# State groups taken in pairs, and projections in whole fp32, in the stage of the states

## What is computed

```python
xn = rmsnorm(h, norm1_g)
proj = xn @ w_in
u, q, k, v, qi, ki, wi, g_ssm, g_attn = split(proj)   # 512, 512, 128, 128, 256, 32, 8, 1024, 1024 columns
# s5_branch: 32 groups of 16 channels and 64 complex states
bu = einsum('gpc,bsgc->bsgp', b_bar, u)
states = associative_scan(a_bar * s + bu)             # over the 256 tokens
y = real(einsum('gcp,bsgp->bsgc', c, states)) + d_skip * u
y = gelu(y); y = y * sigmoid(y @ w_glu)
# dsa_branch: rotation of q, k, qi, ki; then for each token the 64 keys with the highest index score
score = sum_h(relu(qi_h @ ki.T) * wi_h); sel = top_k(score, 64); softmax attention over sel
h = h + (sigmoid(g_ssm) * (y @ w_ssm_up) + sigmoid(g_attn) * (y_attn @ w_attn_up)) @ w_out
```

## Time and profile before

| | us |
|---|---|
| three runs | 1834.30, 1828.82, 1832.76; median 1832.76 |
| the profiled execution | 1834.04, its span 1832.2 |
| granted TensorE clock, mean | 0.967 |
| TensorE matmul / weight load busy | 94% / 82% |
| VectorE, ScalarE, GpSimd busy | 65%, 47%, 41% |
| HBM over the span | 154 GB/s |

### The profile page before, as it was taken

The page is one execution under the profiler, slowest core; times in us unless marked ns, Lnnn a source line. Parts: engine busy times, 40 slices in busy tenths (PEclk is TensorE's granted clock), DMA queues, the critical chain, the costliest instruction groups (busy, mean ns, idle before and its releaser), DMA issues.

```text
span 1832.2 us, 27358 instructions
## 1 busy us (share of the span) xinstructions
PE 1715.8 (94%) x10744; PEld 1505.2 (82%) x10744; DVE 1190.8 (65%) x2438; ACT 864.4 (47%) x1484; POOL 744.2 (41%) x398
## 2 busy tenths in 40 slices
PE   6988999989989998988798999989999999999997
PEld 4766999867789986665578999989999978888886
DVE  7463674745457676678643499989999844444444
ACT  5544666354466644232434345534444445445553
POOL 2323578043246732342445499820000034444442
PEclk9998999999999998989899999999999999999998
DMA  7232554553244554421234365544444556665664
GB/s 279 91 95 88 177 189 167 185 184 104 92 151 173 192 193 169 129 81 58 72 112 174 118 204 182 175 147 142 141 148 139 162 173 194 190 197 188 197 193 138
DMA packets 77457, 283.21 MB, mean 155 GB/s; under 512 B 8721, under 2 KB 8977, under 8 KB 77073
## 3 DMA queue, kind: packets, MB, share of 16 engines
q1 hardware_dynamic: 76032, 276.50, 46.0%
q10 hardware_dynamic: 1296, 4.97, 0.7%
HBM read 279.33 MB, written 2.10 MB: 154 GB/s over the span
## 4 chain that ended last, share of the span: by engine, by line
PE 75%; DVE 16%; issue 3%; ACT 3%; POOL 2%; DMA 1%; POOLq 0%; DVEq 0%; ACTq 0%
PE bank L520 66%; PE bank L511 6%; DVE H L1306 2%; POOL wl L1956 2%; DVE H L1830 1%; DVE H L1836 1%; ACT wh L971 1%; DVE H L1832 1%; DVE H L1834 1%; DVE H L1828 1%; PE bank L800 1%; PE bank L610 1%; DVE wl L1300 1%; DVE gates L1306 1%; DVE ssb L1306 1%
## 5 line engine op out<-in xcount | busy, mean ns | idle before, releaser
L1956 POOL TENSOR_TENSOR wl<-raw,wh 128x1024 fp32r<-128x1024 f32 x227 | 579.1, 2561 | 721.6 <-ACT wh L971 706.7
L971 ACT ACTIVATE wh<-raw 128x1024 fp32r<-128x1024 f32 x515 | 532.7, 1049 | 110.2 <-PE bank L520 99.3
L520 PE MATMUL bank<-hh,wh 128*128 128x256 f32 x1904 | 546.0, 287 | 5.8 <-DVE hl L1306 3.2
L520 PE MATMUL bank<-hl,wh 128*128 128x256 f32 x1904 | 538.6, 283 | 0.0
L520 PE MATMUL bank<-hh,wl 128*128 128x256 f32 x1904 | 537.1, 282 | 0.0
L1300 DVE TENSOR_TENSOR wl<-raw,wh 128x1024 fp32r<-128x1024 f32 (+1 forms) x288 | 385.4, 1344 | 142.9 <-ACT wh L971 142.5
L520 PEld LDWEIGHTS bank<-hh,wh 128*128 128x128 f32 x1904 | 364.6, 191 | 7.9 <-POOL wl L1956 5.3
L520 PEld LDWEIGHTS bank<-hl,wh 128*128 128x128 f32 x1904 | 364.6, 191 | 0.0
L520 PEld LDWEIGHTS bank<-hh,wl 128*128 128x128 f32 x1904 | 364.3, 191 | 0.0
L1306 DVE TENSOR_TENSOR acl<-H,ach 128x256 fp32r<-128x256 f32 x128 | 87.6, 685 | 183.2 <-ACT ach L974 183.2
L520 PE MATMUL bank<-wh,ach 128*128 128x512 f32 x512 | 199.8, 390 | 1.9 <-DVE acl L1306 1.9
(11 more groups left out here) (203 smaller groups left out, 2235.1 us busy)
## 6 DMA issues: line engine op xcount, KB each, us to landing
raw<-in_ut_dram SPq DMA_DIRECT2D x128, 512.0 KB, 3.5
raw<-in_vt_dram SPq DMA_DIRECT2D x128, 512.0 KB, 3.8
raw<-in_wup_dram SPq DMA_DIRECT2D x88, 512.0 KB, 4.0
raw<-in_win_dram SPq DMA_DIRECT2D x48, 512.0 KB, 4.5
raw<-in_wdown_dram SPq DMA_DIRECT2D x44, 512.0 KB, 4.1
raw<-in_wout_dram SPq DMA_DIRECT2D x24, 512.0 KB, 3.6
raw<-in_wga_dram SPq DMA_DIRECT2D x16, 512.0 KB, 3.6
raw<-in_wpq_dram SPq DMA_DIRECT2D x16, 512.0 KB, 4.2
```

The source lines that it names most:

```text
L520: m = p.e.matmul(out, lhs[i][a], rhs[i][b], start=start and i == 0 and j == 0, stop=stop and i == n - 1 and j == 2)
L971: a.e.activation(high_of(u), raw_of(u), ACTF.Copy).then_inc(act_hi.up(("hi", u)), 1)
L1956: g.e.tensor_tensor(low_of(u), raw_of(u), high_of(u).bitcast(F32), ALU.subtract).then_inc(pool_lo.up(("lo", u)), 1)
```

## The change

Three things change, all between the last norm's transposes and the attention over the chosen keys.

1. The units `wu`, `wqkv`, `wqk` and `wga` (29) are no longer split. TensorE reads them from `raw` and multiplies in fp32: one matmul where there were three. The turned activations are copied whole to a new buffer `hw`, half by ScalarE, half by VectorE. `hw` lies where `wh4` and `wl4` lie, so the slots are shifted by two. A slot of these units is free when TensorE has used it.
2. TensorE takes groups in pairs (2m, 2m + 1). The matmuls of the two alternate; their rows (in) or columns (out) of the array start at 32*(n % 4), which differs within a pair. The index scores alternate alike.
3. The order of the loop, now eight pairs with two halves each: TensorE puts `state_out(m - 1)` first, fills, then `state_in(m + 1)`, then turns, scores and fills. VectorE puts the second product of a pair before the first scan; rotations move from n = 5 to the end of pair 2; turns, scores and choice are redistributed (choice 6, 8 and 8 steps in pairs 5, 6 and 7, where it had 2 at n = 10 and 4 at each of 11 to 15).

```diff
-        stage("wu", [(wu_d[n], 1024, True) for n in range(4)])
-        stage("wqkv", quarters(wqkv_d[0]) + quarters(wqkv_d[1]))
-        stage("wqk", [(wqk_d, 320, True)])
-        stage("wga", sum([quarters(wga_d[n]) for n in range(4)], []))
+        stage("wu", [(wu_d[n], 1024, False) for n in range(4)])
+        stage("wqkv", quarters(wqkv_d[0], False) + quarters(wqkv_d[1], False))
+        stage("wqk", [(wqk_d, 320, False)])
+        stage("wga", sum([quarters(wga_d[n], False) for n in range(4)], []))
...
+            whole = first["wu"] <= i < first["wglu"] or first["keys"] <= i < n_early
+            return pe_out if plan[i][2] or whole else dve_out
...
-        FILL = [2, 2, 2, 2, 2, 2, 1, 2, 1, 1, 1, 1, 1, 1, 1, 0]
-        N_ROPE, N_REL = 5, 8
-        Q_TURNS = {7: (8, 6), 8: (0, 2), 9: (4, )}
-        CHOICE = {10: 2, 11: 4, 12: 4, 13: 4, 14: 4, 15: 4}
+        FILL = [(2, 2), (2, 2), (2, 2), (1, 2), (1, 2), (1, 1), (1, 1), (1, 0)]
+        N_ROPE, N_REL = 2, 7
+        Q_TURNS = {(3, 1): (8, 6), (4, 0): (0, 2), (4, 1): (4, )}
+        CHOICE = {5: 6, 6: 8, 7: 8}
...
-        IDX = {9: (0, 1, 2, 3), 10: (4, 5), 11: (6, 7)}
+        IDX = {(4, 1): 0, (5, 0): 2, (5, 1): 4, (6, 0): 6}
...
+                            for k in range(kper):
+                                ready(t, h * kper + k)
+                                m = p.e.matmul(banks[b][:, 0:cw], hTw[:, off + h * kper + k, tcols(t)], unit_whole(i, k, kper, slice(0, cw)),
+                                               start=h == 0 and k == 0, stop=h == nu - 1 and k == kper - 1)
...
+            def state_in(m):
+                pair = (2 * m, 2 * m + 1)
...
                 for j in range(2):
+                    for n in pair:
+                        b, o = 4 + n % 2, 32 * (n % 4)
+                        s = mm(banks[b][:, 256 * j:256 * j + 256], [(BT[o:o + 32, j, n // 4, :], uT[o:o + 32, n // 4, :])])
...
+            def state_out(m):
...
+                p.wait_ge(pool_out, ("prod", 2 * m + 1))
+                for j, (l, a, b) in enumerate(((Cr, 0, 0), (nCr, 1, 1), (nCi, 0, 1), (nCi, 1, 0))):
+                    for n in pair:
+                        o = 32 * (n % 4)
+                        s = p.e.matmul(banks[yb][o:o + 32, 0:256], l[:, 32 * n:32 * n + 32], turned_z[n % 2][:, a, b, :], start=j == 0, stop=j == 3, tile_position=(0, o))
...
             state_in(0)
+            for m in range(8):
+                if m:
+                    state_out(m - 1)
+                for half in range(2):
+                    if half and m + 1 < 8:
+                        state_in(m + 1)
+                    for j in Q_TURNS.get((m, half), ()):
+                        queries_turned(j)
+                    if (m, half) in IDX:
+                        index_scores(IDX[m, half])
+                    for _ in range(FILL[m][half]):
+                        next(fill)
             run(fill)
-            state_out(15)
+            state_out(7)
...
+            for m in range(8):
+                product(2 * m)
+                products_summed(2 * m)
+                product(2 * m + 1)
+                scanned(2 * m)
+                projections(FILL[m][0])
+                products_summed(2 * m + 1)
+                scanned(2 * m + 1)
```

More of the change, by code:

```diff
@@ L198, in program @@
         n_units = len(plan)
-        slot = [i % 6 if i < n_early else (i - n_early) % 4 for i in range(n_units)]
+        slot = [(i + 2) % 6 if i < n_early else (i - n_early) % 4 for i in range(n_units)]
+        assert slot[first["wqkv"]] == 4 == slot[first["wglu"] - 1]
         held, halves_of, before, halved = [], [], {}, {}
@@ L218, in program @@
         J_GATE, N_GR = 57, 64
-        normed = [first["wup", L] for L in range(DEPTH)] + [first["win", 1], first["wu"], first["wpq"]]
+        normed = [first["wup", L] for L in range(DEPTH)] + [first["win", 1], first["wpq"]]
         lower = []
         for i in range(n_units):
-            d2 = first["wga"] - 8 <= i < first["wglu"]
             if i < 6:
@@ L573, in by_features @@
                         claim(b)
-                        m = mm3(banks[b][:, 0:256], [unit_pair(i, k, kt, tcols(c)) for k in range(kt)],
-                                [hT(off + k, ALLC) for k in range(kt)], True, True, ready)
+                        if plan[i][2]:
+                            m = mm3(banks[b][:, 0:256], [unit_pair(i, k, kt, tcols(c)) for k in range(kt)],
+                                    [hT(off + k, ALLC) for k in range(kt)], True, True, ready)
+                        else:
+                            for k in range(kt):
+                                ready(k)
+                                m = p.e.matmul(banks[b][:, 0:256], unit_whole(i, k, kt, tcols(c)), hTw[:, off + k, ALLC], start=k == 0, stop=k == kt - 1)
                         bank_of[tag, c2 * n + c] = b
@@ L755, in pe @@
                     turned(("n", 1), mix, 8, (0,), lambda t: (dve_out, ("nrm", ("n", 1), t)))
-            turned(("n", 2), hn2, 8, (0, 1), lambda t: (dve_out, ("nrm", ("n", 2), t)))
-            by_features("u", first["wu"], 4, 8, 1, 0, ready_both(("n", 2)), lambda c: (act_out if c % 2 else dve_out, ("ev", "u", c)))
+            turned_whole(("n", 2), hn2)
+            by_features("u", first["wu"], 4, 8, 1, 0, ready_whole_both(("n", 2)), lambda c: (act_out if c % 2 else dve_out, ("ev", "u", c)))
             for j in range(2):
@@ L819, in index_scores @@
             def index_scores(i):
[L820 to L823, removed]
+                pair = (i, i + 1)
+                at = [rot(side), rot(side)]
+                for b in at:
+                    claim(b)
                 p.wait_ge(act_out, ("qT2", 6), ("qT2", 8))
                 for s in range(2):
[L826 to L829, removed]
-            state_in(0)
[L832 to L842, removed]
+                    for i, b in zip(pair, at):
+                        t, h = idx_of[i]
+                        nk, o = 128 * t + 128, 32 * h
+                        m = mm(banks[b][:, nk * s:nk * s + nk], [(qT2[o:o + 32, 6 + s, tcols(t)], qT2[o:o + 32, 8, 0:nk])])
+                        if s:
+                            m.then_inc(pe_out.up(("idx", i)), 1)
+                            bank_of["idx", i] = b
+                            emptied[b] = (act_out, ("rel", i))
+            state_in(0)
+            for m in range(8):
[10 more added lines that the diff above has]
+                        next(fill)
             run(fill)
-            state_out(15)
+            state_out(7)
             def glu(n):
@@ L1139, in act @@
             a.e.dma_start(cw, wsm_d[:, 1024:2048]).then_inc(wsc_in.up("wsc"), 16)
-            turned(("n", 2), (0, 1), 2)
+            for t in range(2):
+                a.wait_ge(pe_out, ("T", ("n", 2), t, 0))
+                do(hTw[:, 0:4, tcols(t)], quad(ps("T", ("n", 2), t, 0)), ACTF.Copy, ("hT", ("n", 2), t, 0))
             a.wait_ge(dve_out, ("phase", 1))
@@ L1185, in act @@
             fill = projections()
-            for n in range(16):
-                if n == N_ROPE + 1:
+            for m, half in [(m, half) for m in range(8) for half in range(2)]:
+                if (m, half) == (N_ROPE + 1, 0):
                     a.wait_ge(dve_out, "ropeQ")
@@ L1672, in dve @@
                 stream(first["row", "n", 1] if L == 0 else first["row", "g"])
-            turned(("n", 2), (0, 1), 2)
+            for t in range(2):
+                v.wait_ge(pe_out, ("T", ("n", 2), t, 1))
+                copy(hTw[:, 4:8, tcols(t)], quad(ps("T", ("n", 2), t, 1)), ("hT", ("n", 2), t, 1), alone=True)
             for t in range(2):
@@ L1734, in dve, with product @@
             choice = chosen()
-            for n in range(16):
+            def product(n):
                 cs = tab_s[:, :].rearrange("p (a n t) -> p a n t", a=2, n=16)[:, :, n, :]
```

106 lines of the change are left out of this document (63 added, 43 removed).

## The result

The changed kernel took 1813.3 us (median of four runs, 1806.4 to 1815.2) against 1832.2 us (median of four) for the kernel before, on the same chip. The ratio is 0.988, 95% interval 0.987 to 0.990. The forecast was 1821 us in a range of 1807 to 1831.

A forecast was written before the change was run, and what follows sets the result against it. TensorE and VectorE were taken to bound the stage alternately, VectorE alone from pair 5 in. Stage -9.2, entry -2.4 and behind the stage -1.0 sum to -12.6 us: 1834.0 to 1821.4, stated as 1821, range 1807 to 1831.

The forecast's parts named there:

- The entry: From the last norm to the first state matmul: without splits, root and first projection come earlier, 2.4 us won.
- Units: TensorE's projections: a whole fp32 unit takes 3.45 us where a split one takes 2.9; from above 3.7.
- Rival C: TensorE's projections: each fp32 record's weights aren't loaded beside the matmul before; slower, 1841 us, chance 0.06.
- Pairs: TensorE's state groups: two cost what one did, 1.05 us in and 1.85 out; out bounded by 3.7.
- The walk: The stage timed from first state matmul to last skip: VectorE bounds from pair 5, ends at 139.8 us; before 151.0.
- The collision: Stage's last pair: VectorE's two-input operations alternate with GpSimd's splits for the next stage, each further one costing 2.85 us.
- rival A: Stage's end: VectorE's sums slip in without waiting for GpSimd's splits, or splits aren't ready; 1812 us, chance 0.27.
- The clock's 2 us: TensorE's 40-column unit: its clock may fall to half again, costing between 0 and 3.4 us; 2 taken.
- Behind the stage: After the last skip: a low half of 2.13 us finds GpSimd's splits further on, 1 us won.
- 23 us won by the pairs against 13 lost by the whole units: TensorE's bill over the stage: pairs at 2.9 us replace 5.8; 24 whole units cost 0.55 us more each.

The follow-up runs named there:

- again: The changed kernel run and profiled once more, unaltered: 1812.8 us, ratio 0.988 to the kernel before.
- after: The first profile of the changed kernel, against the kernel before: profiled execution 1806.4 us, span 1804.2 us.
- out_in_turn: Changed kernel, but in a pair out all matmuls of group A go before those of group B: 1819.5 us, ratio 0.993 to the kernel before.
- splits_after_skip: Changed kernel, but GpSimd's splits of the next stage wait for the last skip: 1807.8 us, ratio 0.987 to the kernel before.
- pairs_only: Changed kernel with projections split as before, keeping pairs and the new loop order: 1829.2 us over nine runs, ratio 0.997 to the kernel before.
- choice_between: Changed kernel with 1, 3 and 4 steps of the choice moved between the scans of pairs 5, 6 and 7: 1802.5 us, ratio 0.983.
- fills_late: choice_between with one fill less in each of pairs 3 and 4: 1794.3 us, ratio 0.978 to the kernel before.
- whole_only: Kernel before with whole fp32 projections only, groups one by one in the old order: 1817.9 us, ratio 0.992 to the kernel before.

## Why the prediction was right, and where not

- **The entry.** Forecast -2.4, measured -2.4 (again) and -3.3 (after). GpSimd's timeline of the changed kernel at the entry has no split between the roots, where the earlier trace rows had two in 5.65 us, and the last root waits for VectorE alone:

```profile
704.44 0.55 POOL L2033 TENSOR_TENSOR sta<-sta 128x1 f32<-128x1 f32 x1 [4.43 <-DVE sta L1367]
705.61 0.55 POOL L2033 TENSOR_TENSOR sta<-sta 128x1 f32<-128x1 f32 x1 [0.62 <-DVE sta L1369]
```

- **Units.** Forecast 3.45 us, bounds to 3.7, measured 3.53; the record is 0.441 us, not 0.432. Rival C (weights not loaded beside the matmul) would have made it 0.54.
- **Pairs.** Forecast 1.05 and 1.85, measured 1.06 and 1.85: the unmeasured case, columns side by side, went to the nearer end. Two column tiles gave a factor of 2, where the Trainium skill ("TensorE: Matmul & The Clock Gate", Part 3) gives 2.38 for three; out_in_turn shows the condition that my step left out, the order of issue.
- **The walk.** Pair 5 in at 72.1 us, forecast 72.1. That they are equal is luck: the units cost 1.1 us more than forecast, the turns of the queries 0.9 less (0.80 + 1.02 us). Last pair out over at 126.4, forecast 123.9 (it ran at half clock). VectorE's end 139.0, forecast 139.8, again with errors that cancel. Pair 6 began at 95.2 where I had 93.4, as TensorE twice waited 0.75 us for a copy of ScalarE ahead of pair 4's out, a wait that the walk left out. VectorE's pair took 8.7 us instead of 9.2: of the two sums between the scans only the second was held. A sum beside a split took 2.46 instead of 2.85. The first was held to 849.3, that is 123.1 where I had 122.5.
- **The collision.** VectorE's sums do alternate with GpSimd's splits; rival A, which had them slip in, is dead, and splits_after_skip prices the collision at 7.9 us (forecast 9.4). The Trainium skill ("SBUF — State Buffer", Who interferes with whom) says that a VectorE instruction with two inputs in SBUF contends with a GpSimd instruction that reads SBUF. This trace agrees, with 2.46 us for operations of 0.5.
- **The clock's 2 us: the mis-sized term.** I let the clock fall after the 40-column unit as before. It stayed at 1.00 to 820 us: the unit took 7.20 - 3.53 = 3.67 us. Stage 139.0, where the sum had 142.
- **Behind the stage.** Forecast -1.0, measured -2.0. No experiment separates it further.
- **The end.** 878.4 us instead of 881.1, for which the prediction had no term, nor have I an edit. All kernels with whole units show 878 to 880, pairs_only 884.6. The clock was granted at half for 30.2 us of this part before, for 24.4 in after, 27.7 in again and 33.6 in pairs_only. At half the difference in time, the clock can account for 2.9 of the 3.0 us in after, but only for 1.3 of the 2.7 in again. The rest stays open.

The terms together: the forecast sum was -12.6; measured -19.9, of which -2.8 the stage, -1.0 behind it, -2.7 the end and -0.8 the part ahead are beyond it. The error of 8 us of the median lies there; no mechanism of the sum failed. But the total alone would have misled: 1813.3 us is nearer to rival A's 1812 than to the forecast's 1821. What decides for the forecast is the stage, 139.0 us where A had 130.4, and the stretched sums in its last pair. The -3.5 us of the end and of the part ahead, where no edit was made, were in no term of the forecast; with them the total came near to A's by luck.

One sentence of reasoning did fail, though the total hid it. I wrote the change as 23 us won by the pairs against 13 lost by the whole units. Taken alone, the whole units won 9.7 us of the stage and the pairs 1.8; together 12.0. (By the medians of the whole kernel it is 16.5 and 5.3 us, together 18.9.) The bill of TensorE's costs was right for each, but what a part is worth is decided by the bound that it leaves behind. With the whole units TensorE's holes and its fallen clock were gone. The pairs then made TensorE 21 us lighter (141.3 to 120.4 busy) in a stage that VectorE's order ended, and 2.3 us of them arrived. Where the rest went: VectorE's waits within pairs and the collision. choice_between got 10.8 us of it back, fills_late 9.3 more.

## What to carry to other kernels

Price a part of a change by what is late without it, engine by engine; a split that costs an idle-looking engine little may be what makes holes on the busy one, and unsplitting it can pay although it costs the busy engine more. When one engine has been made much lighter, look next at the order of the others: work that waits for no other engine belongs into their waits, and what they wait for goes ahead of the lighter engine's filler work. Instructions that can share an array must also stand near each other in the queue.

## What was not expected of the hardware

- An instruction for other columns of TensorE starts while earlier ones wait, but not past any number of them: with eight records of group A ahead B started with the fifth, with four ahead at once; a pair out took 2.74, and 1.88 us, where strict alternation took 1.85.
- The granted clock differs between executions of one kernel in a part that no edit touches: it was at half for 27.3 us in after and 44.4 in again. Over the profiles here that part took 702.8 to 710.5 us. A single profile's difference under 8 us says nothing here until it is cut by stretches.
- In whole_only, where TensorE was busy 141.26 of 141.40 us, the clock was 1.00 throughout the stage; with split units and pairs, idle a fifth of the stage, it was 0.87.
